# Sample attention of a decoder layer: queries held still, two half groups, gathered value pages

## The reference

```python
def nsa_sample(...):
    kc = compress(full_rows(pool_kc, kcr), cmp_pe[0], cmp_w1[0], cmp_w2[0])
    vc = compress(full_rows(pool_vc, vcr), cmp_pe[1], cmp_w1[1], cmp_w2[1])
    o_cmp, p_grp = cmp_attend(q, kc, vc, q_pos)
    tok = block_tokens(select_blocks(p_grp, q_pos, PAST_LEN + Q))
    kg = gather_paged(pool_ks, ksr, page_table, tok)
    vg = gather_paged(pool_vs, vsr, page_table, tok)
    o_sel = gathered_attend(q, kg, vg, tok, q_pos)
    o_win = band_attend(q, kw, vw, q_pos, ...)
    out = combine_branches(a_gate, o_cmp, o_sel, o_win)
```

## Time and profile before

| | |
|---|---|
| time of three runs | 1774.44, 1775.79, 1775.86 us (median 1775.79) |
| the profiled execution's own time | 1774.47 us |
| its span, first to last instruction | 1772.8 us |
| PE busy | 1577.5 us, 89% of the span |
| DVE, ACT, POOL busy | 682.0, 292.4, 87.4 us |
| mean granted clock | 0.919 |
| phase sample | about 942 to 1184 us |

### The profile page before, as it was taken

How to read it: one execution, slowest core, us unless ns; L and a number is a source line. 1 busy time by engine, 2 the same in 40 slices (tenths; PEclk the granted TensorE clock), 3 DMA queues, 4 the chain that set the end, 5 groups by cost and what they waited for, 6 DMA issues and landing times.

```text
span 1772.8 us, 26473 instructions
## 1 busy us (share of the span) xinstructions
PE 1577.5 (89%) x11104; PEld 1305.5 (74%) x11104; DVE 682.0 (38%) x1114; ACT 292.4 (16%) x577; POOL 87.4 (5%) x160
## 2 busy tenths in 40 slices
PE   4996699997888698999998997699988999999993
PEld 3874499886666487777767886478877888888883
DVE  3226855335556503433441102301127545554222
ACT  1013101111321001334431011000011111110000
POOL 0000000000000102000002223000000000000000
PEclk9996799998989596999999786799999999999997
DMA  4220000110211247211105563332222222212301
GB/s 152 72 83 25 25 26 16 40 49 16 72 62 36 77 163 156 67 54 54 48 25 167 184 212 121 111 123 78 84 72 80 95 74 93 96 48 99 121 10 49
DMA packets 57082, 143.35 MB, mean 81 GB/s; under 512 B 12050, under 2 KB 31587, under 8 KB 52835
## 3 DMA queue, kind: packets, MB, share of 16 engines
q1 hardware_dynamic: 36722, 97.01, 16.8%
q0 software_dynamic: 14480, 42.02, 7.7%
q10 hardware_dynamic: 5760, 2.62, 0.5%
HBM read 134.11 MB, written 11.65 MB: 82 GB/s over the span
## 4 chain that ended last, share of the span: by engine, by line
PE 84%; DVE 12%; ACT 1%; issue 1%; DMA 1%; POOL 0%; DVEq 0%; SPq 0%; ACTq 0%; POOLq 0%
PE PS L1982 22%; PE PS L238 20%; PE PS L228 11%; PE PS L1627 4%; PE PS L1234 3%; PE PS L1655 2%; PE PS L1713 2%; PE PS L1379 1%; PE PS L254 1%; PE PS L1374 1%; PE PS L1342 1%; PE PS L524 1%; PE PS L536 1%; PE PS L537 1%; PE PS L989 1%
## 5 line engine op out<-in xcount | busy, mean ns | idle before, releaser
L238 PE MATMUL PS<-xyr 128*128 128x260 f32 x1184 | 268.0, 389 | 4.0 <-DVE arena L825 2.5
L238 PEld LDWEIGHTS PS<-xyr 128*128 128x128 f32 x1184 | 228.7, 194 | 40.6 <-DVE arena L825 2.9
L228 PE MATMUL PS<-xyr 128*128 128x260 f32 x896 | 215.3, 393 | 11.0 <-DVE xyr L301 5.8
L228 PEld LDWEIGHTS PS<-xyr 128*128 128x128 f32 x896 | 169.4, 194 | 48.1 <-DVE xyr L301 6.6
L1982 PE MATMUL PS<-arena 128*128 128x260 f32 x638 | 145.1, 383 | 1.5 <-DVE arena L2140 1.3
L1982 PEld LDWEIGHTS PS<-arena 128*128 128x128 f32 x638 | 120.9, 190 | 21.5 <-DVE arena L2140 1.7
L1982 PE MATMUL PS<-xyr 128*128 128x260 f32 x512 | 119.2, 382 | 0.0
L1982 PE MATMUL PS<-arena,xyr 128*128 128x260 f32 x484 | 110.3, 382 | 0.0
L1982 PEld LDWEIGHTS PS<-xyr 128*128 128x128 f32 x512 | 97.3, 190 | 14.9
L1982 PEld LDWEIGHTS PS<-arena,xyr 128*128 128x128 f32 x484 | 92.0, 190 | 14.1
L238 PE MATMUL PS<-arena,xyr 128*128 128x260 f32 x384 | 87.4, 388 | 2.2 <-DVE arena L1920 1.6
(11 more groups left out here) (478 smaller groups left out, 2190.9 us busy)
## 6 DMA issues: line engine op xcount, KB each, us to landing
xyr<-in_w SPq DMA_DIRECT2D x73, 512.0 KB, 3.5
xyr<-in_w_up SPq DMA_DIRECT2D x22, 1024.0 KB, 4.9
arena<-in_pages SPq DMA_DIRECT2D x64, 192.0 KB, 3.6
arena<-in_pages POOLq DMA_DIRECT2D x64, 192.0 KB, 3.8
xyr<-in_w_down SPq DMA_DIRECT2D x10, 704.0 KB, 8.0
xyr<-in_w SPq DMA_DIRECT2D x24, 256.0 KB, 2.7
arena<-in_w_down SPq DMA_DIRECT2D x6, 704.0 KB, 6.0
arena<-in_x POOLq DMA_DIRECT2D x2, 2080.0 KB, 8.6
```

Source lines behind the costliest of these rows:

```text
L228: ins = nc.tensor.matmul(PS[:, 2 * bank + half, 0:HALF], weight(g, k), XN[:, k, half * HALF:(half + 1) * HALF], start=k == 0, stop=k == KT ...
L238: ins = nc.tensor.matmul(PS[:, 2 * bank + half, 0:HALF], weight(g, k), src[:, k0 + k, half * HALF:(half + 1) * HALF], start=first and k == ...
```

## The change

The scores turn round: the queries of a sample become the stationary operand, and the pages the moving one. `QZ` holds for each sample 32 columns, of which its own 8 carry queries and the rest are zero, so that four samples accumulate into one PSUM bank of 32 rows per page group; the four page groups go to the four 32-row strips of the PSUM bank. Samples 0 to 3 and 4 to 7 form two halves, each with its own softmax, over 128 rows (page group and query) instead of a column per query. The first half's softmax is laid between the steps of samples 4 to 7, the second half's between gate products and the values of the first half. The new token's key and value are written into the window tiles and the compressed rows, in the place that is masked before. `AHEAD` = 3 gate products move from merge to sample. The value pages come by one gather of 1 MB per sample on POOL (`indirect_dma_start`, 128 rows of 8 KB), with row numbers that DVE makes once from the page table. `key_pages` reads a sample's eight page numbers first and then waits for the buffer.

```diff
-        plan("merge", [8, 4] * 8)
+        plan("gates", [8] * AHEAD)
+        plan("merge", [4] * AHEAD + [8, 4] * (8 - AHEAD))
...
         def key_pages(queue, b, lane):
 
+            rows_ = [(pg, page(queue, b, pg)) for pg in range(lane, NPAGE, 2)]
             if b >= 2:
                 queue.wait_ge(*at("s_sc_ps", b - 2))
-                queue.wait_ge(*at("s_hid_ps", b - 2))
-            for pg in range(lane, NPAGE, 2):
-                queue.dma_start(PG[b % 2][:, pg], io["pages"][page(queue, b, pg)].rearrange("a p k n -> p (a k) n")).then_inc(
+            for pg, row in rows_:
+                queue.dma_start(PG[b % 2][:, pg], io["pages"][row].rearrange("a p k n -> p (a k) n")).then_inc(
                     *moved("pages", b, lane, lane=2 * lane + b % 2))
...
+        def value_pages(p, b):
 
             if b < NV:
-                queue.wait_ge(*at("s_sc_ps", NS - 2 + b // 3))
+                p.wait_ge(*at("s_sc_ps", NS - 2 + b // 3))
             else:
-                queue.wait_ge(*at("s_pv", b - NV))
...
+                p.wait_ge(*at("s_pv", b - NV))
+            p.indirect_dma_start(VP[b % NV], None, io["pages_v"], bass.IndirectOffsetOnAxis(ap=IDX[:, b:b + 1], axis=0)).then_inc(
...
+                def values(b):
+                    hf, bank_ = b // 4, 3 + b % 2
...
+                    for i in range(NPAGE):
+                        c = i % 4
+                        nc.tensor.matmul(PS[32 * c:32 * c + 32, bank_, 0:128], PT[hf][:, i * 32:i * 32 + 32],
+                                         VP[b % NV][:, i * 128:i * 128 + 128], start=i < 4, stop=False)
...
+                    hf = b // 4
+                    for c in range(4):
+                        ins = nc.tensor.matmul(PS[32 * c:32 * c + 32, 1 + hf, :], QZ[:, b, :], p_[:, 4 * c:4 * c + 4, 2, :],
+                                               start=b % 4 == 0, stop=b % 4 == 3)
+                    pe.wait_ge(*at("s_new_k", b))
...
+                gate_part(0, range(0, 4))
+                compressed(NS - 1)
+                gate_part(0, range(4, 8))
+                cmp_scores(NS - 1)
+                gate_part(1, range(0, 4))
+                pattern(1)
+                gate_part(1, range(4, 6))
+                rank(1)
+                gate_part(1, range(6, 8))
+                values(0)
+                mask(1)
+                values(1)
...
+                    if b == 6:
+                        exp_all(0)
...
+                gate_out(0)
+                exp_cmp(1)
+                gate_out(1)
+                for b in range(4):
+                    heads_out(b)
+                exp_all(1)
+                gate_out(2)
...
+                    if b >= 2:
+                        for x in range(b - 2, b - 1 if b < NS - 1 else NS):
+                            sp.dma_start(VPw[x], io["win_v"][:, x]).then_inc(*moved("windows_v", x, lane=x))
```

More of the change, by code:

```diff
@@ new lines, in max_columns, with sums @@
+                def max_columns(hf):
+                    pe.wait_ge(*at("c_m2", hf))
+                    for c in range(4):
+                        ins = nc.tensor.matmul(PS[32 * c:32 * c + 32, 5, 110:112], M2[0:2, :], id128[0:2, 0:2], start=True, stop=True)
+                    ins.then_inc(*step("pe", "c_maxb_ps", hf))
+                def sums(hf):
+                    pe.wait_ge(*at("c_exp2", hf))
+                    ins = nc.tensor.matmul(PS[:, 5, 114:116], MOD, SUM2, start=True, stop=True)
+                    ins.then_inc(*step("pe", "c_sum_ps", hf))
@@ new lines, in gate_part @@
+                def gate_part(m, ks):
+                    if ks[0] == 0:
+                        if m:
+                            pe.wait_ge(*at("gate_sig", m - 1))
+                        else:
+                            pe.wait_ge(*at("s_x", NS - 1))
+                    part(pe, start["gates"] + m, 0, ks)
+                gate_part(0, range(0, 4))
[3 more added lines that the diff above has]
+                gate_part(1, range(0, 4))
@@ new lines, in pe @@
+                pattern(1)
[5 more added lines that the diff above has]
+                values(1)
+                heads(0)
+                values(2)
+                heads(1)
+                max_rows(1)
+                values(3)
+                heads(2)
+                max_columns(1)
+                heads(3)
+                gate_part(2, range(0, 2))
+                sums(1)
@@ new lines, in dve @@
+                for b in range(NS):
+                    r, n = 32 * (b % 4), b // 4 * 128
+                    v.wait_ge(*at("windows_v", b))
+                    nc.vector.tensor_copy(VPw[b][0:1, 0, :], NVW[r:r + 1, n:n + 128]).then_inc(*step("dve", "new_w", b))
+                compressed(NS - 1)
+                cmp_weights(1)
+                group(1)
+                top(1)
+                masked(1)
+                max_all(1)
+                bias(1)
+                normalise(1)
+                weights_w(1)
@@ L1885, in build, with gate, branch_piece, gate_piece @@
         assert a < TOP - 4680
+        def gate(m):
+            return GATED[m] if m < AHEAD else SG[m % 2]
+        def branch_piece(m):
+            return start["merge"] + (m if m < AHEAD else 2 * m - AHEAD + 1)
+        def gate_piece(m):
+            return start["gates"] + m if m < AHEAD else branch_piece(m) - 1
         class Merge:
@@ L1906, in act @@
             def act(act):
-                for m in range(8):
-                    act.wait_ge(*at("tile", start["merge"] + 2 * m))
-                    if m >= 2:
+                for m in range(AHEAD, 8):
+                    act.wait_ge(*at("tile", gate_piece(m)))
+                    if m >= AHEAD + 2:
                         act.wait_ge(*at("gated", m - 2))
-                    nc.scalar.activation(halves(SG[m % 2]), pair(m % 2), ACT.Sigmoid).then_inc(*step("act", "gate_sig", m))
+                    nc.scalar.activation(halves(gate(m)), pair(m % 2), ACT.Sigmoid).then_inc(*step("act", "gate_sig", m))
                 squares_act(act, "norm2", X2, SQ2t, range(KT), "x2")
@@ L2263, in _ @@
             up_weights(0)
-            for g in range(start["merge"] + RING, len(PIECES)):
+            for g in range(start["gates"] + RING, len(PIECES)):
                 weights_in(g)
```

603 lines of the change are left out of this document (322 added, 281 removed).

## The result

The changed kernel takes 1652.33 us (median of four runs, 1650.53 to 1654.68), the kernel before 1775.19 beside it: a ratio of 0.931 (95% interval 0.929 to 0.933), 122.9 us less. Predicted were 1660, with 1646 to 1705 as the range, and faster at 0.96.

A forecast was written before the change was run, and what follows sets the result against it. PE was taken to bound the kernel, with transfers bounding the new loop. Savings of 100.3 before merge and 14.4 in merge, less 0.3 for constants, gave 114.4 us off 1774.5: 1660 us, range 1646 to 1705.

The forecast's parts named there:

- The bound: Sample loop: PE bound before, with low clock and narrow matmuls; transfers bound it after, 12.0 us a sample instead of 18.1.
- PE per sample, 10.6: Loop: PE's new work per sample sums to 10.6 us at full clock, 13.9 without strip overlap.
- Transfers per sample, 12.0: Loop: 3.67 MB a sample at 310 GB/s takes 11.8 us, about 12.0 with the buffer wait; PE idle 1.4.
- Start, sample 1 at 959: Loop start: sample 1's late pages put its first layer at 959; 2.5 us charged for half clock.
- Behind the loop, 41.6: Between loop and merge: gates, values, small matmuls and waits sum to 41.6 us, so merge starts at 1084.1.
- Merge, minus 14.4: Merge: two more gate products, 64 records, leave it, saving 14.4 us.
- Constants, plus 0.3: Ahead of the first norm: 80 KB more to load at 310 GB/s costs 0.3 us.
- Gathers, nothing: Value gathers on POOL: put at no cost, as eight fit if one takes up to 6.4 us.
- rival 1: Behind the loop: POOL paces the gathers, 1679 us, 1698 by the skill's price, 1755 at the upper bound; chance 0.16.
- Rival 5: Value gathers: slow transfers make the kernel slower than before, about 1934 us, deciding from 20.9 each; chance 0.03.
- Rivals 2 to 4: Loop and values: strips do not overlap, 1699, 0.10; loads keep today's pace, 1697, 0.05; clock falls again, 1714, 0.05.
- Rival 4: Loop: the clock falls again through waits for pages, PE needing up to 21 us a sample, 1714; chance 0.05.

The follow-up runs named there:

- E1: Kernel before, with only the queue's eight page-number reads moved ahead of the buffer wait: 1775.94 us, ratio 1.0007.
- E9: Kernel before, keeping one of 16 narrow score matmuls per sample, the other fifteen left out: 1742.94 us beside 1775.96, one run.
- E2: Changed kernel with page numbers read between the issues again, after the buffer wait: 1661.98 us, ratio 0.936.
- E6: Changed kernel with all window values loaded behind the loop instead of inside it: 1663.71 us, ratio 0.938.
- E7: Changed kernel with sample 1's page numbers read ahead of the phase, POOL issuing its pages before the first window: 1647.44 us, ratio 0.928.
- E12: E7's edit, plus VectorE's row numbers after the queries' copies and sample 0's window behind two pages, against the changed kernel: 1646.20 us, ratio 0.926.
- E4: Changed kernel with one gate product ahead of merge instead of three: 1663.17 us, ratio 0.936.
- E3: Changed kernel with value matmuls ordered strip by strip instead of the four strips in turn: 1662.74 us, ratio 0.936.
- E10: Changed kernel itself, unaltered, timed again beside E7's edit and E12: 1654.29 us, ratio 0.931.
- E5: Changed kernel with each value gather replaced by sixteen plain page issues on POOL: 1756.38 us, ratio 0.9895.
- E8: E6's edit on top of E7's, in the changed kernel: 1657.23 us, ratio 0.933.

## Why the prediction was right

- **The bound.** The forecast was that PE's low clock and narrow matmuls bound the loop, and that pages would bound it next. E1 shows that PE and not the pages' issue bound the old loop, E9, in one run, that the narrow matmuls were most of what was won there. The second half is right in part: with the change the pages' issue does set the pace when it is slower (E2), but 7% fewer bytes win nothing (E6).
- **PE per sample, 10.6.** Sample 7, with all its pages there, takes 10.60. The scores of four strips, where no row showed four, came at 0.90 (predicted 0.88).
- **Transfers per sample, 12.0.** First layers of samples 1 to 7 and the loop's end (959.37 to 1040.15) lie 11.54 apart, 80.8 us in all where 83.5 were forecast. The size is near, the mechanism holds in part. PE was busy for 76.8 of the 80.8, 11.0 a sample and not 10.6, and waited for pages 3.3 in all, 0.5 a sample and not 1.4: less waiting and more work offset each other, which is luck. Pages came at 277 to 335 GB/s, around the row's 310, but not without a gap: from 967 to 971 the transfers stood still for the scores of sample 1, so up to sample 5 the pace was PE's work and the round trip from scores to pages, and from there on PE's, idle for 0.8. The fit of the Trainium skill ("DMA: Bandwidth & Descriptors", anatomy of one DMA on the GpSimd path) made 1652 by way of 10.6 in every sample; here the rate came nearest to its 436 at 412, in sample 7, when gathers of 8 KB rows ran too. The time agrees with it; PE set the pace alone only in the last samples.
- **Start, sample 1 at 959.** It came at 959.37, but the phase began 2.6 us earlier than assumed (939.37 and not 942): 20.0 us into it instead of about 17. So the term was 3 short, and the shift of the phase hid it, which is luck. POOL's issues for it ended at 953.5, 14.1 into the phase (forecast 13.7); the first layer started 5.9 behind them instead of 3.8. The pages of sample 2, released at 950, were on the same engines then; that they are the reason is argued, not shown. E7 and E12 give 3.5 and 6.1 of the wait back.
- **Behind the loop, 41.6.** 40.1. The values of the first four samples are 1.61 to 1.87 apart (predicted 1.6), and PE idles 1.1 us, not 3.0. E4 shows that the cover is real.
- **Merge, minus 14.4.** 15.6 (80.6 from its start to the next product before, 65.0 now): a record took 220 ns, not 224.5.
- **Constants, plus 0.3.** The load right behind them, on which the first norm waits, took 10.84 us against 11.01 before: nothing.
- **Gathers, nothing.** Right, and rival 1 falls: 0.94 of POOL each, near the lower bound of 0.54. The Trainium skill's price of a small read command ("GPSIMD Engine Reference", performance pitfalls), from which the prediction estimated 10.9 a gather, is not what this gather cost. Rival 5 falls by landings of 5.6 to 14.3, under its 20.9.
- **Rivals 2 to 4.** Strips overlap (E3 shows what they cost when they overlap less), loads are faster (E2), and in the profiled execution the clock is low only from 954 to 965, after the start's idle time: the 2.5 charged for it are 2.3 (9.49 against 7.17). Rival 4 is alive in small: in E10, the same kernel, a fall followed a wait for pages, worth 1.7 (8.86 against 7.17).

In sum the sample phase, from its first instruction (941.50 before, 939.37 now) to merge, became 102.1 shorter (242.9 to 140.8; forecast 100.3): 53.1 up to the end of the loop and 49.0 behind it, where two more gate products now stand. Merge became 15.6 shorter (14.4). The remaining 6.3 of the profiled executions' 124.0 lie in code that is the same: 2.1 ahead of the phase, 1.3 behind merge, and 2.9 behind the last store. No term covered them. With the 3.3 that the stages gave beyond the forecast they are the 9.6 us by which the sum, 114.4, fell short of 124.0 (8 by the medians). No run turns the scores round alone or splits the softmax alone: E9 is the nearest to the first, and the 49.0 behind the loop are tested in parts (E3, E4, E5).

## What to carry to other kernels

A matmul that streams 8 columns and loads 128x128 weights keeps PE busy without using it: turning it round gained twice here, by its own time and by the clock of what follows, and putting independent narrow outputs on strips in alternation shortened them once more. The same queue edit is worth nothing or 10 us, depending on which resource is the bound once the rest is in place, so price it against the profile that will be, not the one that is. Bytes taken out of one stage have to be paid where they land; moving them into a stage already full (E6, E8) loses.

## What the runs showed of the hardware that was not expected

- From the end of the last store's issue to the end of the span the kernel before and E1 and E9, built on it, take 13.2 us; the changed kernel and the versions of it take 10.3 to 10.4, E5 10.9. The store is the same. The first three issue transfers from ACT, the others do not; whether that is the cause was not tried.
- The phase begins after 940 us of code that E2 to E6 leave as it is. Among their profiled executions and the two of the changed kernel its start varied from 939.4 to 942.1 us, and these two ends are the same kernel (the first trace and E10); with E7's reads ahead of it, it came as late as 944.1. A term of 2 us can't be read from the end of one trace; it has to be read within its stage.
- Four strips in alternation hid 71% of the serial time of the value matmuls (1.01 of 3.5), and grouped by strip still 35% (2.28).
